# An encoder trunk on one core: squares' statistics inside the last group, the last chunk squared in two halves, the root ahead of a tile

## What is computed

```python
def rmsnorm(x, gain):
    y = x * lax.rsqrt(jnp.mean(x * x, axis=-1, keepdims=True) + EPS)
    return y * gain

for l in range(DEPTH):
    g = norm_gains[l]
    x = x + 0.5 * rmsnorm(swiglu(rmsnorm(x, g[0]), ...), g[1])
    x = x + rmsnorm(mixer(rmsnorm(x, g[2])), g[3])
    x = x + 0.5 * rmsnorm(swiglu(rmsnorm(x, g[4]), ...), g[5])
```

## Time and profile before

| | before |
|---|---|
| median of 3 runs | 2055.05 us |
| lowest, highest | 2051.98, 2055.52 us |
| profiled execution | 2053.03 us, its span 2051.2 us |
| mean granted TensorE clock | 0.999 |
| TensorE matmul busy | 2034.2 us (99%) |
| TensorE weight load busy | 1673.8 us (82%) |
| VectorE, ScalarE, GpSimd busy | 939.7, 713.2, 664.2 us |
| HBM read | 176.18 MB, 87 GB/s over the span |

### The profile page before, as it was taken

One profiled execution on the slowest core, in us unless ns is written; L12 is line 12 of the kernel. 1 busy time (PEld: TensorE's weight loads), 2 busy tenths in 40 slices (PEclk: granted clock), 3 DMA queues, 4 the chain that ended last, 5 costly groups with the idle time before them and its releaser, 6 DMA issues.

```text
span 2051.2 us, 28252 instructions
## 1 busy us (share of the span) xinstructions
PE 2034.2 (99%) x11124; PEld 1673.8 (82%) x11124; DVE 939.7 (46%) x1223; ACT 713.2 (35%) x956; POOL 664.2 (32%) x285
## 2 busy tenths in 40 slices
PE   9999999999999999999999999999999999999998
PEld 7888888878878888888888888878888878888886
DVE  6434331588474433115534311476766776343212
ACT  4222232445342222223322222365655542222221
POOL 3444444220214444441544444200000024444442
PEclk9999999999999999999999999999999999999999
DMA  4322333210122333333233333222221123223332
GB/s 154 103 92 92 100 96 123 93 31 1 61 84 93 92 102 90 95 95 108 75 99 95 92 95 99 83 92 74 73 63 63 63 72 102 93 92 102 89 102 77
DMA packets 51634, 179.46 MB, mean 87 GB/s; under 512 B 5728, under 2 KB 5984, under 8 KB 51552
## 3 DMA queue, kind: packets, MB, share of 16 engines
q1 hardware_dynamic: 51120, 176.73, 27.4%
q10 hardware_dynamic: 432, 1.57, 0.2%
HBM read 176.18 MB, written 2.10 MB: 87 GB/s over the span
## 4 chain that ended last, share of the span: by engine, by line
PE 95%; DVE 3%; ACT 1%; issue 1%; DMA 0%; SPq 0%; DVEq 0%; ACTq 0%
PE psum L599 28%; PE psum L600 27%; PE psum L601 27%; PE psum L755 2%; PE psum L761 1%; PE psum L756 1%; PE psum L984 1%; PE psum L1091 1%; ACT prob L1562 0%; PE psum L708 0%; PE psum L788 0%; PE psum L785 0%; PE psum L1171 0%; PE psum L1128 0%; PE psum L1149 0%
## 5 line engine op out<-in xcount | busy, mean ns | idle before, releaser
L545 POOL TENSOR_TENSOR w_lo<-raw,w_hi 128x1024 fp32r<-128x1024 f32 (+1 forms) x279 | 659.3, 2366 | 1328.5 <-ACT w_hi L1388 1328.5
L599 PE MATMUL psum<-xg_hi,w_hi 128*128 128x512 f32 x1735 | 688.8, 397 | 0.9 <-DVE xg_lo L2184 0.5
L600 PE MATMUL psum<-xg_lo,w_hi 128*128 128x512 f32 x1735 | 679.4, 392 | 0.0
L601 PE MATMUL psum<-xg_hi,w_lo 128*128 128x512 f32 x1735 | 678.6, 391 | 0.0
L1388 ACT ACTIVATE w_hi<-raw 128x1024 fp32r<-128x1024 f32 (+1 forms) x336 | 347.2, 1037 | 852.1 <-DMA raw<-w_up 473.5
L601 PEld LDWEIGHTS psum<-xg_hi,w_lo 128*128 128x128 f32 x1735 | 326.1, 188 | 73.9
L599 PEld LDWEIGHTS psum<-xg_hi,w_hi 128*128 128x128 f32 x1735 | 326.4, 188 | 73.2 <-issue 1.6
L600 PEld LDWEIGHTS psum<-xg_lo,w_hi 128*128 128x128 f32 x1735 | 326.5, 188 | 68.6 <-issue 1.2
L599 PE MATMUL psum<-hid_hi,w_hi 128*128 128x512 f32 x704 | 274.0, 389 | 0.0
L601 PE MATMUL psum<-hid_hi,w_lo 128*128 128x512 f32 x704 | 274.0, 389 | 0.0
L600 PE MATMUL psum<-hid_lo,w_hi 128*128 128x512 f32 x704 | 274.0, 389 | 0.0
(11 more groups left out here) (245 smaller groups left out, 1601.8 us busy)
## 6 DMA issues: line engine op xcount, KB each, us to landing
raw<-w_up SPq DMA_DIRECT2D x176, 512.0 KB, 3.6
raw<-w_down SPq DMA_DIRECT2D x64, 512.0 KB, 3.5
raw<-w_hgrn SPq DMA_DIRECT2D x48, 512.0 KB, 3.6
raw<-w_down SPq DMA_DIRECT2D x32, 384.0 KB, 3.1
raw<-w_mla SPq DMA_DIRECT2D x16, 512.0 KB, 3.6
xt<-x_t SPq DMA_DIRECT2D x8, 256.0 KB, 6.7
out<-xt SPq DMA_DIRECT2D x8, 256.0 KB, 2.2
turned_raw<-w_turned ACTq DMA_DIRECT2D x3, 512.0 KB, 4.6
```

The source lines that it names most:

```text
L545: pool.tensor_tensor(w_lo[slot][:, 0:n], raw[slot][:, 0:n], w_hi[slot][:, 0:n].bitcast(F32), ALU.subtract).then_inc(w_ready, 1)
L599: first = pe.matmul(ps, w_hi[slot][:, at:at + n], hi, start=start, stop=False)
L600: pe.matmul(ps, w_hi[slot][:, at:at + n], lo, start=False, stop=False)
L601: return first, pe.matmul(ps, w_lo[slot][:, at:at + n], hi, start=False, stop=stop)
```

## The change

- `post_statistics` is cut in two. `sum_statistics` holds the four matmuls on `sqsum`; it is now called inside the last group: ahead of the last of 8 blocks for MLA and HGRN (through `final`), ahead of the last three of 22 blocks for an FFN.
- `post_statistics` begins with two unread products (`keep_clock(WHILE_SQUARE)`), then come the four matmuls on `sq`: two after the first half of the square, two after the second. The first of them now frees the last tile's slot.
- ScalarE squares chunk 7 in two halves of 256 tokens. VectorE's copy of chunk 7 waits for both.
- At the borders behind an FFN, the `hi_part` that stood behind the last square now stands behind the root.
- TensorE's loop over the down projection is written out, so that the last group can differ.

```diff
--- before.py
+++ after.py
@@ -106,7 +106,7 @@
 
 N_CHUNK_SIGNALS = 5 * KB + 3 + KB
 
-WHILE_LOADING, WHILE_ROOT, WHILE_CHUNK = 11, 1, 5
+WHILE_LOADING, WHILE_SQUARE, WHILE_ROOT, WHILE_CHUNK = 11, 2, 1, 5
 SUMMED_BY_PE = (0, 1, 2, 3)
 RING = 4
 ENTRY = 4
@@ -639,8 +639,10 @@
                 bank_of_last[0] = ring[(groups[0] - 1) % len(ring)]
                 return psum[:, bank_of_last[0], :]
 
-            def group_into(ps, slot, hi, lo, middle=None, later=None):
+            def group_into(ps, slot, hi, lo, middle=None, later=None, final=None):
                 for k in range(KB):
+                    if final and k == KB - 1:
+                        final()
                     first, last = mm3(ps, (slot, k * P, P), hi[:, k, :], lo[:, k, :], k == 0, k == KB - 1)
                     if k == 0:
                         tile_before_is_free(first)
@@ -666,18 +668,25 @@
                     for _ in ring:
                         group(xg_hi, xg_lo, ring)
 
-            def post_statistics():
+            def sum_statistics():
 
                 pe.wait_ge(sq_added, added.next(KB - 1))
                 for b in range(TB):
-                    first = pe.matmul(psum[:, STAT, b:b + 1], sqsum[:, b * P:(b + 1) * P], ones[:, 0:1],
-                                      start=b == 0, stop=False, skip_group_check=True)
+                    pe.matmul(psum[:, STAT, b:b + 1], sqsum[:, b * P:(b + 1) * P], ones[:, 0:1],
+                              start=b == 0, stop=False, skip_group_check=True)
+
+            def post_statistics():
+
+                keep_clock(WHILE_SQUARE)
+                for b in range(TB):
                     if b == 0:
-                        close(first)
-                pe.wait_ge(sq_ready, squared.next(KB))
-                for b in range(TB):
+                        pe.wait_ge(sq_ready, squared.next(KB))
+                    elif b == TB // 2:
+                        pe.wait_ge(sq_ready, squared.next())
                     last = pe.matmul(psum[:, STAT, b:b + 1], sq[:, (KB - 1) % 2, b * P:(b + 1) * P], ones[:, 0:1],
                                      start=False, stop=b == TB - 1, skip_group_check=True)
+                    if b == 0:
+                        close(last)
                 last.then_inc(stat_done, 1)
                 last_bank.append(bank_of_last[0])
 
@@ -856,7 +865,7 @@
                     group(xg_hi, xg_lo)
                 made = hidden.count
                 hidden.more += FB
-                with loop(pe, KB // 4, (ready, 4 * len(DOWN_PARTS)), (bank_free, 4), stream=stream):
+                for i in range(KB // 4):
                     for j in range(4):
                         ps = open_group(LONG_RING)
                         f = 0
@@ -865,6 +874,8 @@
                             for b in range(blocks):
                                 if j == 0 and (f == 0 or f >= FB - 2):
                                     pe.wait_ge(hidden_ready, made + (f + 1 if f else FB - 2))
+                                if f == FB - 3 and i * 4 + j == KB - 1:
+                                    sum_statistics()
                                 first, last = mm3(ps, (slot, b * P, P), hid_hi[:, f, :], hid_lo[:, f, :],
                                                   f == 0, f == FB - 1)
                                 if b == 0:
@@ -1033,8 +1044,9 @@
                 pe.wait_ge(o_made, MLA_UNITS)
                 output_heads(0, range(HEADS - 2, HEADS))
                 output_heads(1, range(HEADS - 2, HEADS))
-                for _ in range(2, KB):
-                    group_into(open_next(), open_tile(), xg_hi, xg_lo)
+                for j in range(2, KB):
+                    slot = open_tile()
+                    group_into(open_next(), slot, xg_hi, xg_lo, final=sum_statistics if j == KB - 1 else None)
 
             def hgrn():
                 entry((0, 0, 0, 2))
@@ -1324,7 +1336,8 @@
                 pe.wait_ge(o_moved, 1)
                 project()
                 project()
-                project(by_dve=False)
+                slot = open_tile()
+                group_into(open_group(LONG_RING), slot, xg_hi, xg_lo, final=sum_statistics)
 
             pe.wait_ge(zeros_made, 1)
             keep_clock(WHILE_LOADING, t_a)
@@ -1397,7 +1410,9 @@
                 else:
                     out_of_psum.more += 1
                     act.wait_ge(group_done, groups_to_end[0])
-                    src = psum[:, ends[0], :]
+                    for at in (slice(0, SEQ // 2), slice(SEQ // 2, SEQ)):
+                        act.activation(sq[:, j % 2, at], psum[:, ends[0], at], ACT.Square).then_inc(sq_ready, 1)
+                    return
                 act.activation(sq[:, j % 2, :], src, ACT.Square).then_inc(sq_ready, 1)
 
             def take_root(parts, bank=STAT):
@@ -1425,6 +1440,8 @@
                 ends[0] = last_bank[s]
                 if s:
                     take_root([(0, TB, D_MODEL)])
+                    if SUBLAYERS[s - 1][0] == "ffn":
+                        hi_part()
                     wide.more += 1
                     added.more += 1
                 absorbing = SUBLAYERS[s][0] == "mla"
@@ -1502,7 +1519,7 @@
                         for n in range(3):
                             act.dma_start(turned_raw[:, n, :], w_turned[n]).then_inc(turned_in, 16)
                     square_y(j)
-                    if not final or j < KB - 2:
+                    if j < (KB - 2 if final else KB - 1):
                         hi_part()
 
             def output_projection():
@@ -1941,7 +1958,7 @@
                 for j in range(KB):
                     dve.wait_ge(group_done, done.next())
                     if j == KB - 1:
-                        dve.wait_ge(sq_ready, squared.next())
+                        dve.wait_ge(sq_ready, squared.next(2))
                     dve.tensor_copy(y[:, j, :], bank()).then_inc(drained, 1)
                     out_of_psum.more += 1
                     if j == KB - 1:
```

## The result

| | before | changed |
|---|---|---|
| median of 8 runs each | 2054.85 us | 2060.51 us |
| lowest, highest | 2051.97, 2056.31 us | 2059.94, 2062.77 us |
| profiled execution, its span | 2053.03, 2051.2 us | 2059.97, 2058.2 us |
| PE, DVE, ACT, POOL busy | 2034.2, 939.7, 713.2, 664.2 us | 2037.3, 921.5, 713.3, 664.7 us |

What follows compares the result with a forecast made beforehand. 95% of the chain of work that ended last lay on TensorE. Five borders at 0.89 - 0.14 and the one behind HGRN at 1.59 - 0.14 gave +5.2 us on 2053.9: 2059.1 us, range 2053.5 to 2062.5.

Steps and rivals of the forecast that it cites:

- The base that I took, 2053.9: Whole kernel: mean of all four executions of the kernel before, in us, to which the predicted change was added.
- The sum inside the group: Last group before each border: eight one-column matmuls ahead of products cost +0.89 us at each of five borders.
- The halves behind two unread products: Behind the last product: square in two halves brings the root at 2.08 instead of 2.22 us, -0.14 per border.
- The warning that I drew from the Trainium skill: Square's halves on ScalarE: about 0.3 us per ACTIVATE would bring the root hardly earlier, the sum 0.6 us higher.
- The -0.14: Each of six borders: us gained from last product to root by halving the square behind two unread products.
- The root ahead of a tile: Borders behind an FFN: tile rounded after the root is still ready 0.8 us before PE needs it, cost 0.
- The wait behind HGRN: Border behind HGRN: products queue behind the wait for VectorE's addition, +1.59 us instead of 0.89.
- The rest at 0: Later release of the last tile's slot and the written-out down projection loop: each cost 0.
- The 2.5 us for late loads: Borders: term added in the upper end of the range, with a chance of 0.07.
- Rival (a), the clock: Borders: each clock fall avoided returns 1.7 us; one or two falls, chance 0.22; four or more, faster, 0.06.

Runs made afterwards that it cites:

- the pairs: Changed kernel with the sum's matmuls spread over four blocks of an FFN's last group, one pair ahead of each: 2060.02 us in a single run.
- the halves alone: Kernel before with only the last chunk's square in two halves, each waited for: 2053.5 us, ratio 1.0004.
- the thirds: Kernel before with halved square, tile in two pieces, and MLA's 24 one-column matmuls as eight behind each of three blocks: 2050.83 us, ratio 0.999.
- the last pair of kernels: Kernel before with halved square and tile in two pieces, with MLA's 24 one-column matmuls parted into eights or in a row: 2050.83 against 2052.45 us.
- the version in pieces: Kernel before with the square in halves and, behind an FFN, the tile rounded and split in two pieces: 2051.99 us, ratio 0.9993; again 2052.45 us.

## Why the prediction was right, and where it was not

The forecast, 2059.1 us and slower, holds against 2060.51, and +5.2 against the 5.66 between the medians. That closeness is luck. The base that I took, 2053.9, was 0.95 too low, and the code terms sum to +5.2 where the trace shows +8.9; that the clock, which the sum left out, made up for most of it is an argument, and no experiment here measured it. By the steps:

- **The sum inside the group**: +0.89 forecast, 0.90 measured in the changed kernel and in the runs that shared it. The nearest rows were the operation itself at full clock, and the pairs show that nothing of it hides.
- **The halves behind two unread products**: root at S'+2.08, as measured. The warning that I drew from the Trainium skill, "ScalarE: Activation LUTs", section "Rules for kernel authors", is for another case: the page gives its 0.3 us for an ACTIVATE whose bias is a pointer operand, and the profile names no such operand for the squares (their only source is `psum`; the root's are `psum,eps`). They start 0.28 us apart, not some 0.5. The -0.14 itself came at three borders only; behind an FFN the halves alone lost 0.06, since POOL's split of the tile already held the residual step.
- **The root ahead of a tile, "cost 0"**: this step failed, by 3 x 1.41 us alone in the kernel before and by 3 x 1.19 = 3.6 us in the changed one. I asked only whether PE would get the tile in time (it was ready at S'+5.72, forecast 5.87, and that part held). I did not ask what POOL's split now lies over. It stood in the trace before: behind HGRN DVE's addition took 1.34 us, and it ended at 1667.24, 0.55 after POOL's split (row below). Alone it takes 0.69; the 0.85 of the earlier trace rows was held too, by a split that ended at 568.65. In the whole trace before, 119 of VectorE's operations on 512 columns with two SBUF inputs began while a split had more than 0.25 us to go, and every one of them ended 0.5 us or more behind it. With that the step would have read: POOL ends at S'+5.82, the residual step at 6.37 instead of 4.86, +1.5 a border.

```profile
1664.07 2.62 POOL L545 TENSOR_TENSOR w_lo<-raw,w_hi 128x1024 fp32r<-128x1024 f32 x1 [0.20 <-ACT w_hi L1388]
```

- The Trainium skill has the rule, which I did not weigh: "SBUF — State Buffer", section "SBUF: two separate sides", says that VectorE and GpSimd share a pair of ports as an exclusive lock, and that a VectorE operation with two SBUF inputs blocks until GpSimd's is done, if that began first and reads SBUF. The traces agree: the step that reads `t_a` and `xt` is held each time, and L1875, which reads `y` and PSUM, ran beside POOL's split in its usual 0.69.
- **The wait behind HGRN, +1.59**: the mechanism was right, the size was not, 1.05. I took the addition's distance to PE as fixed. It hangs on POOL (1671.37 + 0.55 = 1671.92), and POOL on a tile whose load did not move with PE: that chain came 4.68 us later than before, PE 5.25, so 0.57 less was waited: 1.02 by these rows, near the 1.05.
- **The rest at 0**: in the trace of the changed kernel ACT waits for no load from the last product to the first chunks of the next sub-layer. The 2.5 us for late loads in the upper end of the range, with its chance of 0.07, is a term that no run shows. The loop written out gained nothing that could be seen.
- **Rival (a), the clock**: in part right. The two profiled executions differ by the code's 8.9 us less 1.6 for MLA's fall and 0.4 of small steps. The fall that went was MLA's, 24 us behind a border, and not one of a border's: there the profile shows 24 one-column matmuls in a row in both kernels, at another moment. Six profiles have sixteen one-column matmuls in a row at their borders, and one of those 36 borders fell (the thirds', behind HGRN), so little can have come from breaking these rows up. The medians differ by 1.2 us less than the profiles. The mean granted clock of the changed kernel's runs is 0.999, the kernel before had 0.9978 over 25 other runs, and 0.0012 of 2053 us would be an estimated 2.5 us. But a mean clock can't be turned into time like that: in all eleven profiles the clock also stands at 0.50 for the last 0.7 to 3.8 us of the program, which lowers the mean by up to 0.0009 and costs nothing. So what the clock gave back is between nothing and a few us, and open. That parting the 24 matmuls spares MLA's fall is borne out by the last pair of kernels; why the changed kernel, which still has them in a row, was spared in its profile is open.

Open too is the FFN entry at 590 us, where products came 0.233 apart instead of 0.229 at full clock for some 18 us (+0.35). It turned up behind other borders in other kernels, and in one of the two profiles of the version in pieces and not in the other, so it is a matter of the execution. Its cause was not tried.

## What to carry to other kernels

Before moving an operation to another engine's free time, follow it to what it starts: here a rounding of 1.05 us moved behind the root cost nothing itself, but the GpSimd pass that it releases held VectorE on the critical path for 1.4 us. Look in the trace for the same operation at two durations (0.75 and 0.94, 0.69 and 1.34), and at what ran beside the longer one. And matmuls that fill a wait are free only there: moved into a full stretch, eight one-column matmuls cost as much as four products.

## What the runs showed of the hardware

- A VectorE operation of 128x512 with two SBUF inputs that begins while GpSimd's tensor_tensor runs ends 0.54 or 0.55 us after GpSimd does: POOL's end at S+4.45, 4.52, 4.53, 5.72 and 5.88 gave the step's at 4.99, 5.06, 5.07, 6.27 and 6.42. The profile shows the hold as busy time of VectorE and not as a wait. An overlap of 0.2 us costs the step nothing (0.75 - 0.55). One input in PSUM was not held: 0.69 us beside the split as without it. A copy with one input in SBUF was: `hid_hi` from `t_d`, begun while a split ran, took 2.39 to 2.44 us in the kernel before instead of 0.43 and ended 0.28 after the split.
- A run of eight one-column float32 matmuls among products costs 0.90 us, a pair 0.24.
- The granted clock fell to 0.50 for 3.4 us with PE never idle: in MLA behind 24 one-column matmuls in seven of ten profiles (twice for 6.8 us), and at a border behind sixteen in a row in one. It fell at two borders where sixteen were parted by three products and a wait of 0.75 us. A fall costs 1.6 us among products, and at a border 0.8 once the next groups have given some back. It comes in some executions and not in others: the 25 runs of the kernel before beside the first experiments spread from 2050.9 to 2055.1 us.
